# A gated recurrence inside a fused layer stack: 32x32 blocks at the levels, exponentials in two parts, and five low parts of weights per group on GpSimd

## The reference, cut to what matters

```
u = h @ w_in ; q, a_f, a_b, i, z = split(u, 5)
log_f, key = forget(a, lb)                      # per token and channel, for each direction
b = cumsum(log_f)
scores[t, s] = sum_k q[t,k] * key[s,k] * exp(b[t,k] - b[s,k])     for s <= t (or s >= t backward)
o = scores @ v + (state from earlier chunks)
y = (rms_norm(o_fwd + o_bwd) * silu(z)) @ w_out
```

## Time and profile before

| what | value |
|---|---|
| median of 3 runs | 1928.45 us |
| the profiled execution | 1928.84 us, of which the span of the trace is 1927.0 us |
| TensorE busy | 1920.7 us (100%), 9696 matmuls |
| VectorE busy | 1302.3 us (68%) |
| ScalarE busy | 1076.2 us (56%) |
| GpSimd busy | 556.6 us (29%) |
| TensorE clock granted | 1.00 through the span |

### The profile page before, as it was taken

One profiled execution on the slowest core, in us unless ns is written; L12 is line 12 of the kernel. 1 busy time (PEld: TensorE's weight loads), 2 busy tenths in 40 slices (PEclk: granted clock), 3 DMA queues, 4 the chain that ended last, 5 costly groups with the idle time before them and its releaser, 6 DMA issues.

```text
span 1927.0 us, 26536 instructions
## 1 busy us (share of the span) xinstructions
PE 1920.7 (100%) x9696; PEld 1576.4 (82%) x9696; DVE 1302.3 (68%) x1852; ACT 1076.2 (56%) x1405; POOL 556.6 (29%) x616
## 2 busy tenths in 40 slices
PE   9999999999999999999999999999999999999999
PEld 7888878888888888888887778888888888888887
DVE  5899967546878888887667877555555555544443
ACT  7444466547768696875557775544444444443332
POOL 1899853306060413302401106022222222220000
PEclk9999999999999999999999999999999999999999
DMA  9665656566555555555564445666666666666664
GB/s 322 190 194 178 186 164 198 174 209 184 160 162 164 157 169 160 167 156 180 186 197 141 123 141 189 193 196 192 191 195 186 196 195 195 190 192 196 193 193 161
DMA packets 183152, 352.47 MB, mean 183 GB/s; under 512 B 11792, under 2 KB 12304, under 8 KB 183056
## 3 DMA queue, kind: packets, MB, share of 16 engines
q1 hardware_dynamic: 182912, 351.20, 59.7%
q10 hardware_dynamic: 144, 0.01, 0.0%
HBM read 349.07 MB, written 2.10 MB: 182 GB/s over the span
## 4 chain that ended last, share of the span: by engine, by line
PE 89%; DVE 3%; ACT 3%; POOL 2%; issue 1%; DVEq 1%; POOLq 0%; DMA 0%; ACTq 0%; SPq 0%
PE acc L550 28%; PE acc L552 28%; PE acc L551 28%; POOL kb L467 1%; PE T L660 1%; POOL kf L467 1%; DVEq L1175 1%; ACT E L1002 1%; PE T L509 1%; DVE w_lo L1189 1%; PE T L755 1%; PE T L744 1%; ACT w_hi L797 1%; DVE E L1416 0%; PE T L732 0%
## 5 line engine op out<-in xcount | busy, mean ns | idle before, releaser
L1189 DVE TENSOR_TENSOR w_lo<-raw,w_hi 128x1024 fp32r<-128x1024 f32 x568 | 699.1, 1234 | 533.9 <-ACT w_hi L797 526.1
L797 ACT ACTIVATE w_hi<-raw 128x1024 fp32r<-128x1024 f32 x656 | 688.7, 1057 | 594.7 <-PE acc L552 576.0
L550 PE MATMUL acc<-w_hi,h_hi 128*128 128x512 f32 x1884 | 741.7, 394 | 0.4 <-DVE w_lo L1189 0.2
L552 PE MATMUL acc<-w_hi,h_lo 128*128 128x512 f32 x1884 | 733.7, 389 | 0.0
L551 PE MATMUL acc<-w_lo,h_hi 128*128 128x512 f32 x1884 | 733.6, 389 | 0.0
L550 PEld LDWEIGHTS acc<-w_hi,h_hi 128*128 128x128 f32 x1884 | 353.7, 188 | 80.0 <-issue 5.1
L552 PEld LDWEIGHTS acc<-w_hi,h_lo 128*128 128x128 f32 x1884 | 353.6, 188 | 74.0
L551 PEld LDWEIGHTS acc<-w_lo,h_hi 128*128 128x128 f32 x1884 | 353.9, 188 | 71.2
L498 POOL COPY fT<-fq 32x256 f32<-32x256 f32 x176 | 110.9, 630 | 388.1 <-DVE fq L1651 381.3
L436 POOL TENSOR_TENSOR w_lo<-raw,w_hi 128x1024 fp32r<-128x1024 f32 x80 | 190.4, 2409 | 71.5 <-ACT w_hi L797 71.4
L1269 DVE SCALAR_TENSOR_TENSOR T<-vpad,feat,T 128x256 f32<-128x256 f32 x464 | 182.4, 476 | 0.0
(11 more groups left out here) (245 smaller groups left out, 1581.7 us busy)
## 6 DMA issues: line engine op xcount, KB each, us to landing
raw<-in_hgrn_w_in_dram SPq DMA_DIRECT2D x160, 512.0 KB, 3.7
raw<-in_conv_w_in_dram SPq DMA_DIRECT2D x96, 512.0 KB, 4.1
raw<-in_ffn_w_gate_dram SPq DMA_DIRECT2D x88, 512.0 KB, 4.4
raw<-in_ffn_w_up_dram SPq DMA_DIRECT2D x88, 512.0 KB, 4.2
raw<-in_ffn_w_down_dram SPq DMA_DIRECT2D x88, 512.0 KB, 4.8
raw<-in_attn_w_qkv_dram SPq DMA_DIRECT2D x40, 512.0 KB, 4.0
raw<-in_conv_w_out_dram SPq DMA_DIRECT2D x32, 512.0 KB, 4.6
raw<-in_hgrn_w_out_dram SPq DMA_DIRECT2D x32, 512.0 KB, 4.6
```

Source lines behind the costliest of these rows:

```text
L550: nc.tensor.matmul(o, hi[:, kt, a], w_hi[:, slot, kk, :], start=kt == 0, stop=False)
L552: last = nc.tensor.matmul(o, lo[:, kt, a], w_hi[:, slot, kk, :], start=False, stop=kt == p.chunks * CK - 1)
L797: A(w_hi[:, slot, :, :], raw[:, slot, :, :], ACT.Copy).then_inc(hi_ready, 1)
L1189: TT(w_lo[:, slot, :, :], raw[:, slot, :, :], rounded(w_hi[:, slot, :, :]), ALU.subtract).then_inc(split_ready, 1)
```

## The change

It has three parts.

**Level products of 32x32.** At levels 0 and 3 to 8 the products are cut to 32 keys by 32 queries: 32 products per level, four to each head and block of 128, on output partitions 0, 32, 64 and 96, where there were 16 of 64x64. At level 2 they stay 64x64. Each product of level 3 now pairs a quarter with its neighbour and goes straight to `ST`, so ScalarE's takes at level 3 have another target of the same size; VectorE's masked copies read 256 columns where they read 512, and `blocks` takes four copies where it took two. `SB` and the mask are half as large, with fillers that leave the other tiles where they were.

**Exponentials in two parts.** `diffs` writes the query exponents first and announces them, then the keys' and announces these. `exp` becomes two calls of 128x1024, queries first; TensorE waits for the keys' part on a semaphore of its own, `hgrn_keys`.

**Low parts by GpSimd.** The low parts of chunks 20, 22, 24, 26 and 28 go from VectorE to GpSimd, in groups 1 to 3 of `hgrn` and in `hgrn_z`. GpSimd waits for the low part before it and VectorE, at the next chunk, for GpSimd's.

```
+LEVEL_LOWS = (20, 22, 24, 26, 28)
+def level_low_by_pool(name, j, i):
+    return (name == "hgrn_z" or name == "hgrn" and not is_first(j)) and i in LEVEL_LOWS
...
-        SB = sb(hs, "SB", [P, HPG, 2, P // 2])
+        SB = sb(hs, "SB", [P, HPG, 2, QUARTER])
+        sb(hs, "align_blocks", [P, HPG, 2, QUARTER])
... (GpSimd)
+            def level_lows(name, j):
+                nc.gpsimd.drain()
+                for i in LEVEL_LOWS:
+                    n = ph[name].base(j) + i
+                    slot = i % SLOTS
+                    pool.wait_ge(split_ready, n)
+                    pool.wait_ge(hi_ready, n + 1)
+                    nc.gpsimd.tensor_tensor(w_lo[:, slot, :, :], raw[:, slot, :, :], rounded(w_hi[:, slot, :, :]),
+                                            ALU.subtract).then_inc(split_ready, 1)
+                nc.gpsimd.drain()
             for j in range(4):
+                if j:
+                    level_lows("hgrn", j)
... (TensorE, level)
+                    pe.wait_ge(g_K, 7 * j + s - 1)
...
-                        for i in range(2):
-                            at = (2 * b + i) * HB
-                            to = (2 * b + 1 - i) * HB if s == 2 else at
...
+                        n = HB if s == 2 else QUARTER
+                        for i in range(P // n):
+                            at = b * P + i * n
+                            to = b * P + (i ^ 1) * n if s in (2, 3) else at
+                            g, q = (e[:, 1, h, at:at + n], qT[:, h, to:to + n]) if s == 0 else (e[:, 0, h, at:at + n], e[:, 1, h, to:to + n])
+                            last = nc.tensor.matmul(T[i * n:(i + 1) * n, 2 + s % 2, (2 * h + b) * n:(2 * h + b + 1) * n],
... (ScalarE)
             def exp(j, s):
-                act.wait_ge(g_D, 8 * j + s)
-                e = E[:, (s + 1) % 2, :, :, :].rearrange("p a b c -> p (a b c)")
-                A(e, e, ACT.Exp).then_inc(g_E, 1)
+                for i, done in ((1, g_E), (0, g_K)):
+                    act.wait_ge(g_D, 15 * j + 2 * s - 1 - i)
+                    e = flat(E[:, (s + 1) % 2, i, :, :])
+                    A(e, e, ACT.Exp).then_inc(done, 1)
... (VectorE, stream)
-                    if low_by_pool(ph, n):
+                    if low_by_pool(ph, n) or level_low_by_pool(name, j, i):
...
-                    if isinstance(n, int) and low_by_pool(ph, n - 1):
+                    if isinstance(n, int) and low_by_pool(ph, n - 1) or level_low_by_pool(name, j, i - 1):
                         dve.wait_ge(split_ready, n)
... (VectorE, diffs)
-                TT(gl, rf, kl, ALU.add)
-                TT(gr, kr, rb, ALU.subtract)
                 TT(ql, rb, bl, ALU.subtract)
                 TT(qr, fr, rf, ALU.subtract).then_inc(g_D, 1)
+                TT(gl, rf, kl, ALU.add)
+                TT(gr, kr, rb, ALU.subtract).then_inc(g_D, 1)
```

More of the change, by code:

```diff
@@ L186, in build @@
         ones = sb(mix, "ones", [P, P])
-        lmask = sb(mix, "lmask", [P, len(LEVELS) + 2 - ACT_TAKES, P // 2], I32)
+        lmask = sb(mix, "lmask", [P, len(LEVELS) + 2 - ACT_TAKES, QUARTER], I32)
+        sb(mix, "align_masks", [P, (len(LEVELS) + 2 - ACT_TAKES) * QUARTER])
         wmask = sb(mix, "wmask", [P, 3 * P])
@@ L284, in build @@
             sem(f"hgrn_{s}") for s in ("raw", "quarters", "moved", "act", "lb", "D", "E", "G", "mm", "S"))
-        g_sb = sem("hgrn_blocks")
+        g_sb, g_K = sem("hgrn_blocks"), sem("hgrn_keys")
         g_av, g_o, g_ss, g_std, g_on, g_zr, g_z, g_y, g_yT, g_hi, g_lo = (
@@ L479, in _ @@
                 moves(qT, abtok, range(4)).then_inc(g_M, 1)
+            level_lows("hgrn_z", 0)
             o_power(3)
@@ L986, in cross_keys @@
             def cross_keys(j):
-                act.wait_ge(g_D, 8 * j + 1)
+                act.wait_ge(g_D, 15 * j + 1)
                 for h in range(HPG):
@@ L1007, in take @@
                 if s == 0:
[L1008 removed]
+                    A(SB[:, :, :, :].rearrange("p a b c -> p (a b c)"), T[:, 2, 0:S], ACT.Copy).then_inc(g_S, 1)
                     return
@@ L1015, in take @@
                 c = LEVELS[s - 2]
-                ps = T[:, 2 + s % 2, :].rearrange("p (a c) -> p a c", c=HB)
+                ps = T[:, 2 + s % 2, 0:2 * HPG * c].rearrange("p (a c) -> p a c", c=c)
                 for i in range(P // c):
                     r, o = slice(i * c, (i + 1) * c), (i ^ 1) * c
[L1019 to L1023, removed]
+                    last = A(ST[r, 1, :, :, o:o + c].rearrange("p a b c -> p (a b) c"), ps[r, :, :], ACT.Copy)
                 last.then_inc(g_S, 1)
@@ L1028, in blocks @@
                 act.wait_ge(g_S, 9 * j + 9)
-                for i in range(2):
-                    r = slice(i * HB, (i + 1) * HB)
-                    last = A(ST[r, 1, :, :, i * HB:(i + 1) * HB].rearrange("p a b c -> p (a b) c"),
+                for i in range(4):
+                    r = slice(i * QUARTER, (i + 1) * QUARTER)
+                    last = A(ST[r, 1, :, :, r].rearrange("p a b c -> p (a b) c"),
                              SB[r, :, :, :].rearrange("p a b c -> p (a b) c"), ACT.Copy)
@@ L1425, in take @@
                 V.copy_predicated(SB[:, :, :, :].rearrange("p a b c -> p (a b) c"),
-                                  lmask[:, s - ACT_TAKES, :].unsqueeze(1).to_broadcast([P, 8, HB]),
-                                  T[:, 2 + s % 2, :].rearrange("p (a c) -> p a c", c=HB)).then_inc(g_S, 1)
+                                  lmask[:, s - ACT_TAKES, :].unsqueeze(1).to_broadcast([P, 8, QUARTER]),
+                                  T[:, 2 + s % 2, 0:S].rearrange("p (a c) -> p a c", c=QUARTER)).then_inc(g_S, 1)
             def o_norm(j):
@@ L1675, in constants @@
     i = np.arange(P)
-    k, q = i[:, None] % HB, i[None, :HB]
+    k, q = i[:, None] % QUARTER, i[None, :QUARTER]
     levels = np.stack([(k // (2 * c) == q // (2 * c)) & (k // c != q // c) for c in LEVELS[ACT_TAKES - 2:]], 1).astype(np.int32)
```

2 lines of the change are left out of this document (removed).

## The result

The changed kernel takes 1935.59 us (median of 6 runs, 1934.08 to 1937.18), the one before 1928.34 in the same session (6 runs, 1928.21 to 1928.61). The ratio is 1.0039, 95% interval 1.0027 to 1.0050: slower by 7.3 us, where 11.5 less had been forecast, and outside the range of 1914 to 1922. The profiled execution took 1936.92 us, its span 1935.1.

A forecast was written before the change was run, and what follows sets the result against it. TensorE, busy throughout, was taken to bound the kernel, with VectorE equal to it in the level stretch. From the profiled 1928.84 us, -12.0 + 0.3 gave 1917.1, and 0.4 lower for the median, 1916.8; range 1914 to 1922.

The forecast's parts named there:

- Part 1: 32x32 products at levels 0 and 3 to 8: a burst falls from 1.09 to 0.66 us, 28 save 12.0 us.
- The issue limit: Rival at the bursts: recorded matmuls can't follow faster than some interval; above 17 ns slower, 1943 to 1959 us; chance 0.11.
- part 2: What feeds the bursts: VectorE, ScalarE and GpSimd keep up with TensorE's 6.32 us period; 0.3 us allowed for late feeding.
- the slack: VectorE per level from tick 20 on: 5.3 us of work in TensorE's shorter period, 1.0 us spare.
- The wait is hidden: VectorE's next low part waits for GpSimd's 2.39 us one, covered by 2.41 us of exponents on VectorE.
- only lets part 1 through: Savings on VectorE and in the exponentials have no price of their own; they only let the shorter bursts pay.
- the 0.1 us allowed: ScalarE at each level: one fixed cost more for the second exponential call, about 0.1 us, covered by its 2.94 us wait.
- the allowance of 0.3 us: Level 2, where `weigh` has least cover (0.57 us): 0.1 us lost in each of three stages.
- feeders keep the period: Rival at levels 3 to 8: GpSimd's late low part keeps 6.75 us, only level 0 pays, 1926.8 us; 0.06 including no effect.

The follow-up runs named there:

- the fastest version: The changed kernel with all low parts back on VectorE and TensorE's loop over groups 2 and 3 written out: 1919.80 us, ratio 0.9955.
- the write-only version: The changed kernel with each GpSimd low part replaced by three fills with zeros, these low parts left out of the result: 1920.30 us, ratio 0.9956.
- the copy: The changed kernel with GpSimd's subtraction replaced by a copy of the high part, these low parts left out: 1921.79 us in one profiled run.

## Why the prediction was wrong

**Part 1 was right, its size by a tenth off.** Rounds of four tiles, 16 of them, were put at 0.66 us with the hand-over and are 0.69, so a burst saves 0.39 us (by the distance of the stream's matmuls around it) instead of 0.43, and 28 save 10.9 instead of 12.0. A window of 10 ns at the start shows four in flight:

```profile
508.77:508.78 0.01, 0.01 (x4) 0.01 (x4) 1.00 1.57 614
```

The issue limit falls: 64 recorded matmuls in 0.69 us are 11 ns each. (The prediction prices the same 25 ns a matmul once at 17 us and once at 14; 0.5 us a burst, 28 times, is 14, and 17 comes out only with 0.12 us more per burst.) The page "TensorEngine Tiling (Array Packing)" of the Trainium skill, section "Instruction Overhead", would have made it an estimated 1.6 us if its 60 cycles held for every matmul in turn; the trace says that they do not, with four tiles side by side.

**The step that failed** is this one of part 2: "VectorE's own instructions may stretch beside a busy GpSimd: 1.44 us against 1.22, 0.2 or 0.4 us a period, inside the slack." It is 2.2 us (2.88 against 0.68), sixteen times in the four stages. The rest of the sum was good: VectorE's period was put at 5.3 us, and 7.42 less 2.2 is 5.2. The slack was there, 1.1 us (6.34 less 5.2), and the stretch is twice that. TensorE waits from level 6 on, 0.8 to 1.5 us more ahead of each burst than usual, 13.1 us over twelve bursts. Level 5 is spared because the cover built up before it (1.4 us) is used up there first.

I had read a rate where the hardware has an exclusion. Rows 15 is a low part beside GpSimd's block moves, which are short, about 0.6 us each. That an instruction which has to let one of them pass loses little fits this, though no run isolates it. The right row was in the trace of before, in the convolution stage. VectorE and GpSimd:

```profile
L1303 DVE TENSOR_TENSOR cy<-cy,ln_rstd x8: 679/684/2110, 274.3 to 294.9; 128x512 f32<-128x512 f32 x8
```

```profile
273.44 2.39 POOL L436 TENSOR_TENSOR w_lo<-raw,w_hi 128x1024 fp32r<-128x1024 f32 x1 [2.50 <-ACT w_hi L797]
```

Eight like instructions, two operands each, and the one that starts inside GpSimd's low part (at 274.27) takes 2110 ns instead of 684 and ends 0.55 us behind it. A median hides it, the maximum shows it. The Trainium skill has the rule on its page "SBUF — State Buffer", section "Who interferes with whom": the two engines share a port pair as an exclusive lock, and a VectorE instruction with two SBUF inputs contends with a GpSimd instruction that reads SBUF, not with one that only writes. The runs agree on each point: 2.88 us beside a read of two operands, 1.53 beside a shorter read of one, 0.68 beside writes alone, transposes with one operand unchanged.

**"The wait is hidden"** (VectorE's next low part waits for GpSimd's) was right at ticks 20 to 26. At tick 28 there are only transposes to hide it, and VectorE waits 3.4 us in all, in three of the stages; with one low part at 28 alone the kernel loses about 1 us.

**The split of the exponentials** was called something that "only lets part 1 through", and so it is, shown from both sides. That the low parts were needed as well was wrong: the narrower masked copy brings VectorE to 6.36 us a level in the fastest version (a low part at 521.18 and the next at 527.54), TensorE's period there is 6.34 (bursts at 515.52 and 521.86), and the cover in hand lasts to level 8. The second call costs ScalarE more than the 0.1 us allowed: from the start of the exponential to the next instruction it is 2.17 us at levels 5 to 8 instead of 1.82, and ScalarE still waits for VectorE ahead of it (1.7 to 3.3 us at levels 6 to 8).

**Not foreseen: the code, and the starts of the stages.** Stalls outside the bursts grew by 6.3 us in the profiled execution. Of these 2.6 are TensorE's stall behind its loop's jump (671.58 - 668.76, less the usual 0.23) and 1.6 the slower clock behind it (eleven matmuls in 4.10 us instead of 2.50). The queue that brings instructions, on the page after:

```profile
q8 instruction: 73, 1.20, 0.3%
```

Before it had 58 packets and no stall, and the kernels with the loop and 64x64 products have none either. 224 more recorded matmuls a group are the likely reason, and writing the loop out removes the stall, though the queue then still has 70 packets: the number of packets alone doesn't explain it. As TensorE would have waited a few ticks later anyway, the medians give 1.4 and 0.5 us for it, not 4.2. The remaining 2.1 us lie at the starts of stages, ticks 3 to 14, where ScalarE and GpSimd's moves set the pace: a part of what the bursts save is given back there (one wait is 0.90 us, up to 581.75, for VectorE's low part). This is read from the traces; no run isolates it. The fastest version shows the same: its bursts save 10.9 us, its time only 8.7. So the allowance of 0.3 us stood at the wrong place (level 2), and should have been about 2.

**The sum again**: -10.9 (bursts) + 13.1 (exclusion) + 6.3 (code, clock, starts) = 8.5 us, and the four stages are 8.5 us longer; the profiled executions differ by 8.1. The rival "feeders keep the period" had the place right and the cause wrong: not a late low part but VectorE itself standing, and so it could end on the slower side, which I had given to the issue limit alone. The slower clock makes up a part of the spread between runs of versions with the loop: the two of the changed kernel whose mean granted clock is 0.999 took 1936.9 and 1937.2 us, the four at 1.000 took 1934.1 to 1936.1; without low parts the two at 0.999 took 1922.4, the three at 1.000 1920.6 to 1921.2. What stays open is why it follows the stall in some executions (in the profiles: this one, that of the write-only version and that of the copy) and not in others (that of the version without low parts).

## What to carry to other kernels

Before work that reads SBUF goes from VectorE to GpSimd, list what VectorE runs beside it. If that has two operands in SBUF, the move costs most of GpSimd's duration, here 2.2 us for 1.13 saved; beside one-operand work it cost only the wait here. Look at the longest of a group of like instructions, not at its median, to see whether two engines exclude each other. And where two loops of work have the same period, price a gain only once both are shortened: here products or exponentials alone gave nothing that could be measured, both 8.7 us.

## What the runs showed of the hardware

- VectorE with two SBUF operands and GpSimd reading SBUF exclude each other for whole instructions: a VectorE instruction of 0.68 us ends 0.55 us after GpSimd's, at all 52 such places of four kernels (16 in the changed one, 16 with the low parts alone, 16 with the copy, 4 with one low part at tick 24). It then takes 2.88 us beside a subtraction and 1.53 beside a copy. GpSimd loses too: 2.4 us become 2.7 to 3.3 when it starts inside a VectorE instruction of that kind. Beside GpSimd that only writes the exponents keep their 0.68 us, and VectorE's transposes, with one operand, keep 1.30 for two beside GpSimd's subtraction.
- 64 recorded 128x32 matmuls with 32 output partitions, in plain 32-bit floats, take 0.69 us to the next matmul at the full clock, 11 ns each, four in flight.
- With 224 more recorded matmuls in its body, TensorE's loop had a stall of 2.3 to 2.5 us at the jump in all four profiles that have both, and none in the five with the loop written out. In three of the four the clock fell to the lower level behind it, 0.52 granted over 3.3 us in that of the changed kernel.
